# Hybrid attention/SSD/MoE layer on one core: token table made earlier, order of three GpSimd steps changed

## The reference, cut to what matters

```
scores = sigmoid(t @ w_router)                      # 512 tokens x 64 experts
idx    = top 8 experts of each token (4 of 8 groups allowed)
gates  = the 8 scores, normalised, x 2.5
routed = sum over experts: (silu(t @ w_eg[e]) * (t @ w_eu[e]) * gate) @ w_ed[e]
shared = (silu(t @ w_sg) * (t @ w_su)) @ w_sd
out    = x + g2 * (routed + shared)
```

## Time and profile before

| | before |
|---|---|
| median of 3 runs | 1822.55 us (1822.4 to 1825.23) |
| the profiled execution | 1824.93 us, of it span 1823.2 us |
| PE busy | 1572.7 us (86%) |
| DVE busy | 1312.5 us (72%) |
| ACT busy | 935.9 us (51%) |
| POOL busy | 288.1 us (16%) |
| the loop over experts | from 1053 us to about 1750 us of the span |
| DMA in that loop | mostly 340 to 380 GB/s |

### The profile page before, as it was taken

How to read it: one execution, slowest core, us unless ns; L and a number is a source line. 1 busy time by engine, 2 the same in 40 slices (tenths; PEclk the granted TensorE clock), 3 DMA queues, 4 the chain that set the end, 5 groups by cost and what they waited for, 6 DMA issues and landing times.

```text
span 1823.2 us, 22784 instructions
## 1 busy us (share of the span) xinstructions
PE 1572.7 (86%) x7266; PEld 1226.2 (67%) x7267; DVE 1312.5 (72%) x1672; ACT 935.9 (51%) x1152; POOL 288.1 (16%) x280
## 2 busy tenths in 40 slices
PE   6899889899898998999897579999997799999950
PEld 1676676687677676677676467877775678877730
DVE  2695856466765867867758768888885549888849
ACT  2335536433343343342522267888885558887730
POOL 2000000000200201001003422322222213222210
PEclk9899999999999999999997789999998889999985
DMA  8122121264333233221532369999996759999948
GB/s 286 53 88 70 47 70 47 78 211 139 110 99 116 75 99 115 93 69 47 196 125 81 143 234 347 376 373 361 359 382 249 270 193 382 367 357 349 345 171 359
DMA packets 108834, 361.43 MB, mean 198 GB/s; under 512 B 19932, under 2 KB 30368, under 8 KB 81856
## 3 DMA queue, kind: packets, MB, share of 16 engines
q1 hardware_dynamic: 81120, 295.20, 44.0%
q0 software_dynamic: 22688, 45.29, 6.7%
q10 hardware_dynamic: 4928, 19.78, 2.7%
HBM read 352.18 MB, written 43.66 MB: 217 GB/s over the span
## 4 chain that ended last, share of the span: by engine, by line
PE 55%; DVE 18%; DMA 15%; ACT 5%; issue 5%; SPq 1%; ACTq 0%; POOLq 0%; POOL 0%; DVEq 0%
PE psum L1494 15%; PE psum L1496 14%; PE psum L1495 14%; DMA rawm<-in_w_exp_up 9%; PE psum L860 2%; DVE ofin L1112 2%; DVE ring L1029 2%; DMA rawm<-in_w_exp_down 2%; PE psum L1527 2%; DVE cv L2052 2%; ACT ring L952 1%; ACT hl L1276 1%; PE psum L1688 1%; PE psum L1741 1%; DMA xo<-h_rows,oix 1%
## 5 line engine op out<-in xcount | busy, mean ns | idle before, releaser
L1029 DVE TENSOR_TENSOR ring<-rawm,ring 128x2048 fp32r<-128x2048 f32 x189 | 429.7, 2287 | 42.6 <-ACT ring L952 42.1
L952 ACT ACTIVATE ring<-rawm 128x2048 fp32r<-128x2048 f32 x189 | 362.3, 1918 | 78.3 <-DMA rawm<-in_w_exp_up 40.7
L1494 PE MATMUL psum<-ring,xT 128*128 128x512 f32 x528 | 224.0, 424 | 26.2 <-DVE ring L1029 21.1
L1827 DVE TENSOR_TENSOR hl<-raw,hl 128x2048 fp32r<-128x2048 f32 x59 | 135.0, 2292 | 116.9 <-ACT hl L1276 116.4
L1496 PE MATMUL psum<-ring,xT 128*128 128x512 f32 x528 | 210.9, 399 | 0.0
L1495 PE MATMUL psum<-ring,xT 128*128 128x512 f32 x528 | 210.3, 398 | 0.0
L1494 PE MATMUL psum<-hl,hT 128*128 128x512 f32 x416 | 170.1, 409 | 6.4 <-DVE hT L2132 3.6
L805 POOL DMA_INDIRECT y_rows<-yb,row_of x64 | 100.0, 1563 | 434.4 <-ACT yb L994 418.9
L1495 PE MATMUL psum<-hl,hT 128*128 128x512 f32 x416 | 164.5, 395 | 0.0
L1496 PE MATMUL psum<-hl,hT 128*128 128x512 f32 x416 | 164.1, 395 | 0.0
L1494 PEld LDWEIGHTS psum<-ring,xT 128*128 128x128 f32 x528 | 101.9, 193 | 54.0 <-DVE ring L1029 21.8
(11 more groups left out here) (374 smaller groups left out, 2948.2 us busy)
## 6 DMA issues: line engine op xcount, KB each, us to landing
rawm<-in_w_exp_down SPq DMA_DIRECT2D x64, 1024.0 KB, 9.8
rawm<-in_w_exp_gate SPq DMA_DIRECT2D x64, 1024.0 KB, 12.1
rawm<-in_w_exp_up SPq DMA_DIRECT2D x64, 1024.0 KB, 15.0
raw<-in_w_in SPq DMA_DIRECT2D x36, 1024.0 KB, 5.1
modraw<-in_w_ada SPq DMA_DIRECT2D x64, 256.0 KB, 2.9
ysum<-y_rows ACTq DMA_DIRECT2D x16, 1024.0 KB, 8.9
raw<-in_w_ada SPq DMA_DIRECT2D x8, 1024.0 KB, 9.6
raw<-in_w_branch_b SPq DMA_DIRECT2D x8, 1024.0 KB, 5.5
```

The lines of the kernel that those rows point to most:

```text
L952: A(ring[:, slot, 1, :], rawm[slot][:], ACT.Copy).then_inc(S["m_hi2"], 1)
L1029: TT(ring[:, slot, 0, :], rawm[slot][:], ring[:, slot, 1, :].bitcast(F32), ALU.subtract).then_inc(S["m_lo2"], 1)
L1494: M(dst, lhs(0), rhs(0), start=first, stop=False)
L1827: TT(hl[:, slot, 0, :], raw[slot][:], hl[:, slot, 1, :].bitcast(F32), ALU.subtract).then_inc(S["lo_done"], 1)
```

## The change

Three edits:

1. In the list of steps, only the first half of the shared tile `out(x, 2)` now stands ahead of `route` and `pos` of the second half of the tokens; before it was one and a half tiles (all of tile 2, half of tile 3). `counts` moves from behind `sact` to right behind `slots`.
2. `gates` of the second half leaves the list; DVE now makes `tok_of` first, then the three `first_lo`, then `gates`, then the low part of the first transposed rows. Before, `first_lo(0)` and `first_lo(1)` stood ahead of `tok_of`.
3. In POOL's turn e, `more(e)` and `first_more_rows(e + 1)` now stand ahead of `scatter(e - 1)`.

```diff
     item("lgB", 1)
     out(x, 1, ui=1)
     sgu1 = steps[-1]
-    out(x, 2)
+    out(x, 2, ui=0)
     item("route", 1)
-    out(x, 3, ui=0)
     item("pos", 1)
     pos1 = steps[-1]
     item("slots", 1)
-    out(x, 3, ui=1)
+    item("counts", 0)
+    out(x, 2, ui=1)
+    out(x, 3)
     item("xhi", 2)
     item("sact", 0)
-    item("counts", 0)
-    item("gates", 1)
...
                     gather(e + 3)
-                if e:
-                    pool.wait_ge(S["y_ev"], e)
-                    scatter(e - 1)
                 if e < NE:
                     more(e, counts)
                 if e + 1 < NE:
                     counts = first_more_rows(e + 1)
+                if e:
+                    pool.wait_ge(S["y_ev"], e)
+                    scatter(e - 1)
...
-            first_lo(0)
-            first_lo(1)
             v.wait_ge(S["table_in"], 16)
             V.tensor_single_scalar(tok_of[:], row_of[:], 3, ALU.arith_shift_right).then_inc(S["tok_ready"], 1)
+            for n in range(3):
+                first_lo(n)
+            gates(v, L, 1)
...
-            first_lo(2)
             v.wait_ge(S["xt_hi"], 1)
             x_lo(0).then_inc(S["xt_lo"], 1)
```

## The result

The changed kernel takes 1814.89 us (median of 8 runs, 1812.38 to 1817.79) against 1823.67 us of the kernel before beside it (8 runs, 1819.95 to 1828.34): ratio 0.9948, 95% interval 0.9936 to 0.9960, so 8.8 us less. Its profiled span is 1811.3 us, 11.9 less than before's.

The account below looks back on a forecast made before the run. PE, busy 86% of the span, was taken to lose time waiting for rows POOL fetches (17.9 and 13.4 us). Terms 4.0 + 9.4 + 1.9 - 0.5 = 14.8 us off 1822.55 gave 1808 us, range 1802 to 1817.

Parts of the forecast that it names:

- The table and `tok_of`: Ahead of the loop: `slots` 4.35 us sooner, `tok_of` 7.6 us sooner, PE newly waiting 0.9 us for DVE.
- What is late next: Start of the loop: the gather lands slower among loads, so the first low part gains 4.0 us of 7.6.
- The extra rows: Two extra bodies of crowded experts: earlier fetch ends PE's waits 4.8 and 4.6 us sooner, 9.4 us.
- The clock: Extra transposes in both extra bodies come before PE's clock falls to half: 0.9 us each, 1.9 us.
- What the move costs: Scatter now behind the extra-row fetch, its transfer after the restart: 0.5 us lost for both bodies, bounds 0 and 1.4.
- supply takes it back: Rival for the whole loop: loads set the pace, only the start counts, 1818.5 us; chance 0.10.
- The start brings nothing: Rival at the loop's start: gather still behind 5 MB of loads, loop starts at 1053 again, 1811.8 us; chance 0.15.
- The fetch isn't sooner: Rival in POOL's turn: something else ahead holds the extra-row fetch, only the start counts, 1818.5 us; chance 0.03.
- slower: Rival after extra bodies: the gather behind the late scatter lands too late, 1828 us if 10 us late twice; chance 0.04.
- The clock stays up: Rival in the extra bodies: PE keeps full clock there, 8 us more gain, 1800 us; chance 0.08.

Follow-up runs that it names:

- e1: Kernel before with only edit 3, POOL's extra-row fetch ahead of the scatter: 1823.1 us against 1828.0, ratio 0.9974.
- e10: Kernel before with only POOL's read of the next expert's counts moved ahead of the scatter: 1825.2 us against 1825.6, ratio 1.0001.
- e5: The changed kernel measured again, unaltered: 1821.7 us against 1826.7 of the kernel before, ratio 0.9973.
- e9: Changed kernel plus an unused read of the counts between POOL's scatter and gather: 1817.2 us against 1825.6 of the kernel before, ratio 0.9957.
- e2: Changed kernel with POOL's old turn, so edits 1 and 2 alone: 1823.0 us against 1828.0 of the kernel before, ratio 0.9975.
- e6: Changed kernel with SP's first two loads for expert 2 held until the first gathered rows land: 1816.6 us against 1826.7 of the kernel before, ratio 0.9942.
- e3: Kernel before with edit 1 alone, the order of `tok_of`, `first_lo` and `gates` as before: 1826.3 us against 1828.0, ratio 0.9989.
- e4: Changed kernel with `tok_of` put behind the three `first_lo` and `gates`: 1825.0 us against 1828.0 of the kernel before, ratio 0.9986.
- e12: e11 plus the unused read of the counts between scatter and gather: 1811.4 us against 1825.6 of the kernel before, ratio 0.9918.
- e8: Changed kernel with PE's wait for `y_ev` in the extra body moved to ahead of its down product: 1818.1 us against 1826.7 of the kernel before, ratio 0.9943.
- e7: e6 with `gates` of the second half put back behind `sact`: 1817.8 us against 1826.7 of the kernel before, ratio 0.9937.
- e11: Changed kernel with the additions of e6, e7 and e8 together: 1811.6 us against 1825.6 of the kernel before, ratio 0.9926.

## Why the prediction was right, and where not

The forecast was 14.8 us off; the measured time is 8.8 us off, and 5.0 in the repeat. The time of 1814.9 us lies in the range up to 1817, and the direction and the places of the gain were right; two terms were too large. There is luck in it: 8.8 is just inside of the 8.6 to 17.4 that the terms' bounds gave, and the repeat's ratio (0.9973) on the 1822.55 us that the forecast started from would be 1817.6, outside of the range.

**The table and `tok_of`: right.** With 2.43 us taken off, the forecast put `slots` at 1001.9 (measured 1001.85), the issue of `row_of` at 1028.4 (1028.64), `tok_of` at 1036.2 (1035.98). The new wait of PE was 0.86 us (0.9).

**What is late next: right.** The landing was put at 1049, 9.2 us behind the issue, and took 10.1; 4.0 us of gain were expected, 3.4 measured in this profile and 3.6 between the means (74.5 in before, e1 and e10; 70.9 in the change, e5, e9 and e2). `gates` was covered. The rule of the Trainium skill that was weighed there (DMA: Bandwidth & Descriptors, Queues, rings and completion order) is that each DMA engine takes packets in turn from the queues that have work. The short landing that the prediction read out of it did not come. With 2 MB of the loads held back it took 7.7 us (e6), so the loads ahead are a cause; how the DMA engines shared their time no run shows.

**The extra rows: the step that failed.** The 9.4 us were 4.8 and 4.6; measured are 3.3 and 2.2 (means of four executions with the old order, 18.5 and 14.4 us into the turn, and seven with the new, 15.2 and 12.2). The prediction named the next condition, `y_ev`, rightly, and took the time at which it was met before. Left were waits of 4.7 and 2.4 us instead of 3.1 and 1.1. Three things were missed. `y_ev` itself comes 1.1 us later, because ACT stands ahead of it waiting longer for down weights (e1, e2). That the fetch among them is what delays them was not tested. PE starts 0.3 us behind the end of ACT's copy. And the profile of before had one of the longer second waits: 15.1, where e2 and e3 with the same order had 13.7 and 13.3. The fetch itself was issued 4.0 us behind the gather and not 2.5, since its index copy took 2.12 us (0.20 in before), beside a low part on DVE; as `y_ev` was what PE waited for, that cost nothing.

**The clock: half right.** 0.9 us for each body were expected. The first extra transposes still ran at half clock (1.97 us, after 4.66 us of idle time), and the first body gained no more than its wait: 3.4 us (39.3 to 36.0). The second ran at full clock in five of the seven, and the second body gained 3.4 us (45.7 to 42.3), 1.2 more than its wait. 0.5 of the 1.2 are in the turn itself and 0.7 in the turn behind it, which the prediction had not counted; that turn was a short one, at granted clock 1.00, in one of the four executions with the old order and in five of the seven with the new. The idle time just before the transposes doesn't sort them: with the old order they ran at full clock after 4.23 us (e2) and 3.83 (e3), with the new at half after 2.06 (e4) and 2.50 (e9).

**What the move costs: within its bounds.** 0.5 us were taken, with 0 as the lower bound. The scatter behind the extra body cost nothing that the trace shows: the two turns after the first body took 20.23 us against 20.21, and PE never waited for `xg` there.

**Sum, with what was measured:** 3.6 + 3.4 + 3.4 = 10.4 instead of 14.8.

**Of the rivals,** "supply takes it back" leaves only the start and gave 1818.5, 4 us off. The repeat alone (5.0 off) can't exclude it. e1 can: with the start as before, POOL's order alone took 4.9 us off (2.2 to 7.3), where this rival has nothing. "The start brings nothing" falls with e2 (2.0 to 7.1 us off). "The fetch isn't sooner" falls with its issue at 1377.13, and "slower" with the missing waits for `xg`. "The clock stays up" falls with a granted clock of 0.50 in the first extra body (1395 to 1400) and 0.55 in the second (1446 to 1450).

Yet between 10.4 and the measured 5 to 9 something is missing. In turns 7 to 33 the four executions with the old order of POOL took 259.6 us in the mean (258.2 to 261.0), the ten with the new 261.5 (259.7 to 263.4). That would be 1.8 us back. The table sorts them better: the three executions with the table as before (before, e1, e10) are the three shortest of all fourteen, 258.2 to 259.7 with a mean of 258.9, and the eleven with edit 1 took 259.9 to 263.4, mean 261.5. That would be 2.5 us lost again of what the table gained, as the supply rival has it, but only for this part. It isn't the earlier start of the loop, for e4 started late and took 262.2; of the spacing of gather and scatter, e10 speaks against it. Both groupings were made after the fact, and with a scatter of 1.3 us from one execution to the next the smaller one may be chance. **This stays open.**

## What to carry to other kernels

When a wait is taken off, the next condition must not be read at its old time: ask what it hangs on, and whether the transfer that was moved lands among what it waits for (here a delay of 1.1 us went with the move, its cause only argued). A gather issued sooner into a deep queue of loads lost about half of that time again in its landing (4.3 of 7.7 us); hold back the loads that aren't needed yet. And one profile is one draw: a wait that hangs on a landing varied here by 2 us from execution to execution, so price it from several. And look in the trace whether an experiment's edit moved what it was meant to move: e9 and e12 left the spacing where it was.

## What the runs showed of the hardware

- The first gather, from issue to PE's use of its rows: 10.0 to 10.3 us with 5 MB of loads and writes issued around it (the changed kernel, e2, e5, e8, e9), 6.6 to 7.7 us with 3 MB (e6, e7, e11, e12), 5.3 us behind them (e4). The changed kernel issues it 5 us behind the first of the 5 MB; issued 10 us behind (e3) it took 7.6, and 12 us behind (before) 5.8.
- DMA issues of POOL were held while DVE made a low part from two large SBUF operands. In the fourteen traces every gather, scatter or fetch in the loop that began during such a DVE instruction (2.2 to 2.3 us each; over 900 cases) ended 0.8 to 1.0 us behind the end of that instruction. Those with DVE idle took 0.96 to 1.05 us. The first gather took 2.23 us beside L1016 and 1.05 us in e4, where DVE was idle.
- The turn behind an extra body has two lengths: 9.4 us where the granted clock of its first 6 us was 1.00, and 10.9 to 11.0 us where it was 0.72 to 0.74. Both occurred with either order.
- The kernel itself varies: the unchanged marker lay at 979 to 987 us over fourteen executions, and the same pair of kernels gave ratios of 0.9948 and 0.9973 in two measurements whose intervals only touch.
